# Rotary scores of the first block in one term instead of two, with the key rotation and three evacuations moved

## The reference, cut to what matters

```python
def apply_rope(x, cos, sin):
    x1, x2 = xf[..., :half], xf[..., half:]          # half = 32
    return concatenate([x1 * cos - x2 * sin, x2 * cos + x1 * sin], -1)

q_rope = apply_rope(q[..., NOPE_DIM:], cos, sin)     # (seq, 8 heads, 64)
k_rope = apply_rope(k_r, cos, sin)                   # (seq, 64), shared by the heads
s = (einsum('bqhd,bkhd->bhqk', q_nope, k_nope)
     + einsum('bqhd,bkd->bhqk', q_rope, k_rope)) * ATTN_SCALE
pr = softmax(where(mask, s, -1e30)); out = einsum('bhqk,bkhd->bqhd', pr, v)
```

## Time and profile before

| what | value |
| --- | --- |
| median of 3 runs | 2095.64 us (2095.04 to 2097.87) |
| the profiled execution | 2094.94 us, of which the span of the trace is 2093.1 us |
| PE busy | 2037.7 us (97% of the span) |
| DVE busy | 1420.3 us (68%) |
| ACT busy | 1065.9 us (51%) |
| mean granted clock of PE | 0.993 |
| DMA queue q1 | 383.87 MB, 54.0% of 16 engines' span |

### The profile page before, as it was taken

One profiled execution on the slowest core, in us unless ns is written; L12 is line 12 of the kernel. 1 busy time (PEld: TensorE's weight loads), 2 busy tenths in 40 slices (PEclk: granted clock), 3 DMA queues, 4 the chain that ended last, 5 costly groups with the idle time before them and its releaser, 6 DMA issues.

```text
span 2093.1 us, 37177 instructions
## 1 busy us (share of the span) xinstructions
PE 2037.7 (97%) x14556; PEld 1883.8 (90%) x14556; DVE 1420.3 (68%) x1860; ACT 1065.9 (51%) x1370; POOL 9.8 (0%) x16
## 2 busy tenths in 40 slices
PE   9999999999999999999999999999999998999998
PEld 8999998899999999999899999797888787778877
DVE  5556767565567555777565557666799776767986
ACT  5444544454447444544444446535677544646774
POOL 1000000000000000000000000000000000000000
PEclk9999999999999999999999999999999999999999
DMA  8555564355555555465245555343799443036992
GB/s 293 180 180 181 161 201 142 105 167 183 183 186 161 184 183 183 154 202 178 85 154 188 181 182 194 112 136 121 274 363 362 172 155 102 1 141 251 366 364 105
DMA packets 89664, 388.08 MB, mean 185 GB/s; under 512 B 10096, under 2 KB 10096, under 8 KB 74832
## 3 DMA queue, kind: packets, MB, share of 16 engines
q1 hardware_dynamic: 88992, 383.87, 54.0%
q0 software_dynamic: 560, 2.67, 0.3%
HBM read 385.45 MB, written 1.05 MB: 185 GB/s over the span
## 4 chain that ended last, share of the span: by engine, by line
PE 87%; DVE 7%; ACT 3%; issue 2%; DVEq 1%; DMA 0%; ACTq 0%; SPq 0%
PE psa L1812 59%; PE psd L1812 19%; PE psa L2082 2%; DVEq L1066 1%; DVE w_lo L1081 1%; PE psd L2108 1%; PE psd L1982 1%; PE psd L2091 1%; PE psd L2027 0%; DVE w_lo L1076 0%; PE psd L1854 0%; PE psa L2001 0%; DVE x_lo L1094 0%; PE psa L2027 0%; PE psd L1950 0%
## 5 line engine op out<-in xcount | busy, mean ns | idle before, releaser
L1081 DVE TENSOR_TENSOR w_lo<-raw,w_hi 128x1024 fp32r<-128x1024 f32 x500 | 589.3, 1220 | 124.9 <-ACT w_hi L720 122.5
L1812 PE MATMUL psa<-x_hi,w_hi 128*128 128x256 f32 x1680 | 481.9, 287 | 15.1 <-DVE x_lo L1094 5.8
L1812 PE MATMUL psa<-x_lo,w_hi 128*128 128x256 f32 x1680 | 477.3, 284 | 0.0
L1812 PE MATMUL psa<-x_hi,w_lo 128*128 128x256 f32 x1680 | 477.2, 284 | 0.0
L720 ACT ACTIVATE w_hi<-raw 128x1024 fp32r<-128x1024 f32 x250 | 263.1, 1052 | 328.2 <-PE psa L1812 304.4
L1812 PEld LDWEIGHTS psa<-x_hi,w_hi 128*128 128x128 f32 x1680 | 324.2, 193 | 20.9 <-DVE x_lo L1094 7.9
L1812 PEld LDWEIGHTS psa<-x_lo,w_hi 128*128 128x128 f32 x1680 | 324.3, 193 | 0.3
L1812 PEld LDWEIGHTS psa<-x_hi,w_lo 128*128 128x128 f32 x1680 | 324.4, 193 | 0.0
L1812 PE MATMUL psa<-y_hi,w_hi 128*128 128x256 f32 x1008 | 284.8, 283 | 6.4 <-DVE w_lo L1081 2.9
L1812 PE MATMUL psa<-y_lo,w_hi 128*128 128x256 f32 x1008 | 284.8, 283 | 0.0
L1812 PE MATMUL psa<-y_hi,w_lo 128*128 128x256 f32 x1008 | 284.8, 282 | 0.0
(11 more groups left out here) (401 smaller groups left out, 3518.4 us busy)
## 6 DMA issues: line engine op xcount, KB each, us to landing
raw<-weights SPq DMA_DIRECT2D x500, 512.0 KB, 4.8
raw<-weights SPq DMA_DIRECT2D x60, 1024.0 KB, 6.1
raw_y<-weights SPq DMA_DIRECT2D x36, 1024.0 KB, 6.0
x<-weights SPq DMA_DIRECT2D x18, 1024.0 KB, 4.9
h<-x_in SPq DMA_DIRECT2D x1, 1024.0 KB, 4.8
result<-h SPq DMA_DIRECT2D x2, 512.0 KB, 2.9
sml<-smalls POOLq DMA_DIRECT2D x1, 831.0 KB, 10.5
cst<-consts POOLq DMA_DIRECT2D x1, 751.5 KB, 7.8
```

Source lines behind the costliest of these rows:

```text
L1081: dve.tensor_tensor(w_lo[:, s, c], raw[:, s, c], w_hi[:, s, c], ALU.subtract).then_inc(lo_done, 1)
L1812: ins = pe.matmul(out, lhs, rhs, start=first and n == 0, stop=last and n == 2, skip_group_check=True)
```

## The change

One half of the rotary key's features now stands beside the other on the partitions, so that a head's 64 rotary features make one term. Unit `kr` has one block of 128 columns (first half twice, second half twice); `low(3)` writes it, and a copy with the two halves exchanged through two operations over 64 partitions. `k_rot` has 2 slots. The key is rotated between the g_conv and the g_mla units with two products and four sums. `query(0)` writes each of its two sums in two parts of 64 partitions, one of which lands on the other half's partitions. The copies of `n0`, `n1` and `K` move from DVE to ACT, with a semaphore of their own. In ACT's attention loop (MLA and NSA) the copy of the turned probabilities of item t - 2 stands ahead of the exponential of item t.

```diff
-                  unit(np.concatenate([np.tile(kr[:, :half], (1, 4)), np.tile(kr[:, half:], (1, 4))], 1))]
+                  unit(np.concatenate([np.tile(kr[:, :half], (1, 2)), np.tile(kr[:, half:], (1, 2))], 1))]
...
-        k_rot = view(11276, 8, T)
+        k_rot = view(11276, 2, T)
...
                 for t in range(items + 4):
+                    if 0 <= t - 2 < items:
+                        act.wait_ge(t_done, seen.more(t_done))
+                        act.activation(probs_t[t % 2], psd[:, t % 2, 0:384], ACT.Copy).then_inc(pt_ready, 1)
                     if t < items:
                         act.wait_ge(nmax_ready, seen.more(nmax_ready))
...
-                    if 0 <= t - 2 < items:
-                        act.wait_ge(t_done, seen.more(t_done))
-                        act.activation(probs_t[t % 2], psd[:, t % 2, 0:384], ACT.Copy).then_inc(pt_ready, 1)
...
-                units(3 + 1 + 1 + 2)
+                units(1)
+                units(2, lambda j: act.activation(q_n[:, 4 * j:4 * j + 4, :], four(j), ACT.Copy).then_inc(act_evac, 1))
+                units(1, lambda j: act.activation(keys_n, psd[:].rearrange("p a (b t) -> p (a b) t", b=2),
+                                                  ACT.Copy).then_inc(act_evac, 1))
+                units(1 + 2)
...
-                low_rank = [(q_c[:, 0:2, :], 2), (q_c[:, 2:3, :], 1), (kv_c, 2), (k_r, 2)]
+                low_rank = [(q_c[:, 0:2, :], 2), (q_c[:, 2:3, :], 1), (kv_c, 2), (k_r[:, 0:1, :], 1)]
+                first, second = slice(0, P // 2), slice(P // 2, P)
...
+                    if j == 3:
+
+                        for to, part in ((second, first), (first, second)):
+                            dve.tensor_tensor(k_r[to, 1, :], pair(j)[part, 0, :], rstd[part], ALU.mult)
...
                 mark(for_act)
+                dve.wait_ge(act_out, seen.more(act_out))
+
+                dve.tensor_tensor(rope_a[:, 0, :], k_r[:, 0, :], cos1, ALU.mult)
+                step(dve.tensor_tensor(rope_a[:, 1, :], k_r[:, 1, :], sin1, ALU.mult))
+                for j, combined in enumerate((ALU.subtract, ALU.subtract, ALU.add, ALU.add)):
+                    r = slice(32 * j, 32 * j + 32)
+                    ins = dve.tensor_tensor(k_rot[r, j % 2, :], rope_a[r, 0, :], rope_a[r, 1, :], combined)
+                step(ins)
                 units(4, lambda j: times_rstd(g_mla[:, 2 * j:2 * j + 2, :], pair((2 + j) % 4)))
...
-                    step(dve.tensor_tensor(q_rot[:, 0:2, :], rope_a[:], rope_b[:], ALU.subtract))
+                    turned_q = q_rot.rearrange("p (i e) t -> p i e t", e=2)
+
+                    def combine(to, combined):
+                        for e, part in enumerate((first, second)):
+                            ins = dve.tensor_tensor(turned_q[to, :, e, :], rope_a[part], rope_b[part], combined)
+                        return ins
+                    step(combine(first, ALU.subtract))
...
-                    return dve.tensor_tensor(q_rot[:, 2:4, :], rope_a[:], rope_b[:], ALU.add)
-                units(3, query)
-                units(1, lambda j: dve.tensor_copy(keys_n, psd[:].rearrange("p a (b t) -> p (a b) t", b=2)))
+                    return combine(second, ALU.add)
+                units(1, query)
+                units(3, None)
...
-                for j, n in enumerate((2, 1, 2, 2)):
+                for j, n in enumerate((2, 1, 2, 1)):
...
-                            (q_rot[:, t // 4, q], k_rot[:, 2 * (t % 4), 0:keys]),
-                            (q_rot[:, 2 + t // 4, q], k_rot[:, 2 * (t % 4) + 1, 0:keys])]
+                            (q_rot[:, t // 2, q], k_rot[:, t % 2, 0:keys])]
```

More of the change, by code:

```diff
@@ L560, in two_blocks @@
         heads_read = sem("heads_read")
+        act_evac = sem("act_evac")
         h_scaled, r_scaled = sem("h_scaled"), sem("r_scaled")
@@ L1323, in _ @@
                 split_x([(0, 4)], conv_c, x_hi, x_lo)
[L1325 to L1335, removed]
                 def query(j):
-                    if j > 0:
-                        return dve.tensor_copy(q_n[:, 4 * j - 4:4 * j, :], four(j - 1))
                     c = cos1.unsqueeze(1).broadcast_to([P, 2, T])
@@ L1344, in query @@
                     step(dve.tensor_tensor(rope_b[:], r2, s, ALU.mult))
-                    step(dve.tensor_tensor(q_rot[:, 0:2, :], rope_a[:], rope_b[:], ALU.subtract))
+                    turned_q = q_rot.rearrange("p (i e) t -> p i e t", e=2)
[4 more added lines that the diff above has]
+                    step(combine(first, ALU.subtract))
                     dve.tensor_tensor(rope_a[:], r2, c, ALU.mult)
                     step(dve.tensor_tensor(rope_b[:], r1, s, ALU.mult))
-                    return dve.tensor_tensor(q_rot[:, 2:4, :], rope_a[:], rope_b[:], ALU.add)
-                units(3, query)
-                units(1, lambda j: dve.tensor_copy(keys_n, psd[:].rearrange("p a (b t) -> p (a b) t", b=2)))
+                    return combine(second, ALU.add)
+                units(1, query)
+                units(3, None)
                 units(1, lambda j: dve.tensor_copy(vals, psa[:].rearrange("p (a b) t -> p a (b t)", a=2)))
-                dve.wait_ge(act_out, seen.more(act_out))
+                dve.wait_ge(act_out, seen.more(act_out, 2))
                 units(2, lambda j: dve.tensor_tensor(merged[:, 4 * j:4 * j + 4, :], four(j, psd),
@@ L2152, in _ @@
                     columns([block_of(b0 + i) for i in range(4)], 3, y, 4)
-                    pending.append(evac)
+                    pending.append(act_evac)
                 settle(2)
                 columns([block_of(b, psd) for b in range(KD)], 2, y)
-                pending.append(evac)
+                pending.append(act_evac)
                 settle(1)
```

## The result

The changed kernel takes 2076.32 us (median of 4 runs, 2075.59 to 2076.47) against 2095.44 for the kernel before beside it (2095.04 to 2097.87): a ratio of 0.9906, 95% interval 0.9889 to 0.9923, or 19 us less. The forecast was 21.7 us less, 2073.9, with a range of 2068 to 2080.

The account below looks back on a forecast made before the run. PE's own work, 87% of the chain, was taken to bound the kernel. Savings of 5.76 + 3.0 + 1.48 + 10.0 + 1.5 = 21.7 us, taken from the median, gave 2073.9 us, range 2068 to 2080.

Parts of the forecast that it names:

- 1, `kr`: Low-rank stage: one block less, 24 matmuls, saves PE 2.88 us in each layer, 5.76 us for both.
- 2, rotation moved: Key rotation behind the last g_conv unit: 2.5 us of DVE work hidden in 2.97 us idle, 0.4 in hand.
- 3, n1 and K: PE's wait at n1 goes, one of some 2.1 us at K stays; K starts 1.50 us earlier each layer, 3.0 in all.
- the rival of dear sums: At K: four partial sums at double price, giving 2079.5 us; chance 0.08.
- 4, clock: Unit K: with one wait in place of two it takes 6.03 us in both layers, saving 1.48 us.
- 5, copies to ACT: Copies of n0, n1 and K: moving them to ACT is worth nothing, being covered by PE's work.
- 6, MLA: MLA attention: shorter head terms and the copy's new place save 5.02 us a layer, 10.0 us for both.
- The rival by which ACT and DVE bound the shorter head: MLA and NSA: the copy's new place doesn't shorten the loop, heads go at about 2.8 us, 2078.0 us; chance 0.13.
- 7, NSA: NSA attention: the earlier copy frees the reduction held behind `y_lo`, saving 1.5 us, bounds 0 and 3.0.
- The clock falls again: At unit K: half clock again in layer 0, or in both, giving 2075.4 to 2076.9 us; chance 0.10.
- the main case: Whole kernel: the forecast as worked out, within 2 us, range 2071 to 2077; chance 0.50.

Follow-up runs that it names:

- Experiment 4: Changed kernel with unit K's split on DVE ahead of the query rotation, PE writing K's banks 2 and 3 first: 2068.43 us.
- Experiments 5: Changed kernel with PE computing unit kr's one block a second time, 24 matmuls more in each layer: 2079.52 us.
- experiment 6: Changed kernel with PE computing half of unit kr's block again, 12 matmuls more in each layer: 2077.02 us.
- experiment 2: Kernel before with only ACT's copy of the turned probabilities moved ahead of the exponential: 2090.30 us.
- Experiment 3: Changed kernel with the rotary term of each MLA score added twice, PE's work in a head back to 12 records: 2082.18 us.
- experiment 7: Changed kernel with PE filling its wait for unit K with nine matmuls over zeros into a free bank: 2070.88 us.
- experiment 1: Changed kernel with ACT's copy of the turned probabilities back behind the exponential: 2080.48 us.

## Why the prediction was right, and which terms were not

**1, `kr`: right.** 2.88 a layer. The 2.31 us in hand for unit v were in truth 1.54: DVE was still splitting another unit (until 227.08) when `kr` was done. I had let its chain start with the result; it cost nothing.

**2, rotation moved: right,** with 0.25 us in hand for 0.4.

**3, n1 and K: right.** The wait at n1 is gone, K starts 1.51 and 1.52 earlier (1.50 said), the wait there is 2.13 (2.1 said). Each pair of partial sums took 1.38 to 1.39 (1.40 said): operations that go to other partitions than the one ahead don't overlap with it, and have no other price. So the rival of dear sums was wrong. Experiment 4 shows what was late next as the prediction named it, K's split behind `query(0)`: with the split moved the wait is gone.

**4, clock: wrong.** "I take 6.03 for both: 1.48 us." K took 7.46 and 7.51: nothing gained in layer 0, 1.48 lost in layer 1, 2.96 off. The step took one longer wait for milder than two shorter ones. The runs show it the other way: behind the single wait K fell to the half clock eight times in ten, behind the two once in four, which are few cases. The same step left out that the other waits of the program stand in another place in time after the change: 12 stretches of half clock where there were 8, another 2.06 + 0.76 = 2.8 us in stretches whose instructions are unchanged. Experiments 5 and 6 show that such stretches come and go while the waits stay, experiments 2 and 3 that they do so even where nothing ahead of them was changed, experiment 7 that K no longer falls when its wait is filled. Why just those stretches fell stays open.

**5, copies to ACT: right** as far as it shows: V and the projection follow K without idle time. The copy of `n1` ends at 323.28, while PE waits for K's split and 1.07 before K starts, and that of `K` at 333.72 under unit V. The copies' move alone was not tried.

**6, MLA: right.** 5.17 and 5.15 a layer for 5.02. Experiment 3 gives the term's worth (4.79 for 4.65), experiment 1 the copy's place (1.33 and 1.31 a layer, with the loop of 2.80 from the prediction). In the longer head of the kernel before that place is worth only 0.39 (experiment 2), and 4.79 + 0.39 is again 5.18. The rival by which ACT and DVE bound the shorter head is just what experiment 1 makes of the kernel, and the changed kernel escapes it by the copy's move.

**7, NSA: right in its mechanism, mis-sized.** 1.5 was said, 4.0 measured. The sum counted only the reduction behind `y_lo`. It left out that PE's weighing waited for the copied probabilities after every pair of transposes that had come late themselves: 2 x 0.20 us a group, in eight groups 3.2 us at most. These waits stood in the list of waits as 16 short ones of PE's weight loads.

The errors are of opposite sign: NSA +2.5 and MLA +0.3, clock -2.96 and -2.8, the start -0.3. 21.7 + 2.8 - 6.1 = 18.4, against 18.6 of the span. That the total came within 2.4 us of 2073.9 is therefore in part luck: what the clock took was made up in half by what NSA gave beyond its term. At K the rival *The clock falls again* came true, in both layers, and it had 0.10. The total lies in the 2071 to 2077 of the main case, but not within the 2 us that the prediction set beside it.

## What to carry to other kernels

Where a stage alternates between engines, take from the trace the loop that each engine would run alone and set the shortened one against the next: here 2.455 against 2.43 after, 2.80 without the reordering. Judge an edit by the length of its stages in the chain as well as by the total, since half-clock stretches came and went by four between these kernels in code that was not changed, and some did so between executions of the same code. A short wait ahead of a stage can be worth more than its length: moving the split (experiment 4) gave 7.9 us for two waits of 2.13, and filling them with matmuls over zeros (experiment 7) 5.4 without making K start earlier.

## What of the hardware was not expected

Extra work can be almost free: 2.88 us more of PE's work cost 0.7 us (experiment 6), and its profiled execution has 8 stretches at half clock where the changed kernel's has 12. That the shift of the waits did this is not shown. Two equal waits of 2.1 us ahead of the same 48 matmuls gave 7.51 us once and 6.02 once in one execution, and in layer 0 of two executions, with the same code up to there, 7.46 and 6.02. I know of no row that tells ahead which of them falls; that stays open.
